# The up stage of a decoder-layer kernel: x1 added late, gathered rows kept out of the first and last round, the final norm in two combined passes

## The reference

```python
# x1: the layer's state after the first sublayer and its norm
def token_block(args):
    xb, eb, gb = args
    act = jax.nn.gelu(jnp.einsum('pd,phkd->phk', xb, expert_down[eb]).astype(f32), approximate=False)
    return jnp.einsum('phk,phkd->pd', (gb * act).astype(x.dtype), expert_up[eb])
# x <- LayerNorm(alpha * x1 + PEER(x1)), alpha = 2 ** 0.25, eps 1e-5
```

## Time and profile before

| | us |
|---|---|
| median of 3 runs | 4306.57 |
| lowest and highest of the 3 | 4306.22 and 4308.96 |
| profiled execution | 4310.81 |
| its span, first to last instruction | 4309.0 |
| TensorE busy | 3957.7 (92%) |
| VectorE busy | 2586.9 (60%) |
| mean granted TensorE clock | 0.958 |

### The profile page before, as it was taken

One profiled execution on the slowest core, in us unless ns is written; L12 is line 12 of the kernel. 1 busy time (PEld: TensorE's weight loads), 2 busy tenths in 40 slices (PEclk: granted clock), 3 DMA queues, 4 the chain that ended last, 5 costly groups with the idle time before them and its releaser, 6 DMA issues. The chain is left out here.

```text
span 4309.0 us, 61280 instructions
## 1 busy us (share of the span) xinstructions
PE 3957.7 (92%) x21744; PEld 3573.4 (83%) x21744; DVE 2586.9 (60%) x5114; ACT 1367.3 (32%) x2139; POOL 1702.3 (40%) x1159
## 2 busy tenths in 40 slices
PE   9999994996888788998999999999988999999996
PEld 7888884886888666998999999999976888888885
DVE  2154102554555334116777888886648888898888
ACT  2133221652222211112472644635512222222220
POOL 0000003624444004000727656566626555555556
PEclk9999996997999899999999999999999999999998
DMA  3223224642222322223549779698888888888884
GB/s 132 97 88 106 94 86 129 160 109 71 76 75 84 138 95 94 88 68 129 136 139 318 231 227 299 201 331 278 262 315 289 289 291 290 285 290 298 280 289 185
DMA packets 390923, 801.82 MB, mean 186 GB/s; under 512 B 65265, under 2 KB 204401, under 8 KB 389745
## 3 DMA queue, kind: packets, MB, share of 16 engines
q1 hardware_dynamic: 280176, 531.25, 36.9%
q0 software_dynamic: 110592, 268.62, 19.9%
HBM read 623.40 MB, written 154.32 MB: 180 GB/s over the span
## 5 line engine op out<-in xcount | busy, mean ns | idle before, releaser
L1935 PE MATMUL r_psd<-x1h,r_dh 128*128 128x384 f32 x2048 | 700.9, 342 | 19.0 <-DVE r_dl L1733 19.0
L1935 PE MATMUL r_psd<-x1l,r_dh 128*128 128x384 f32 x2048 | 688.4, 336 | 0.0
L1935 PE MATMUL r_psd<-x1h,r_dl 128*128 128x384 f32 x2048 | 688.3, 336 | 0.0
L2180 PE MATMUL e_psy<-e_uh,e_Ch 128*128 128x512 f32 x1536 | 600.1, 391 | 36.3 <-DVE e_Cl L2105 31.9
L2180 PE MATMUL e_psy<-e_ul,e_Ch 128*128 128x512 f32 x1536 | 599.5, 390 | 0.0
L2180 PE MATMUL e_psy<-e_uh,e_Cl 128*128 128x512 f32 x1536 | 599.4, 390 | 0.0
L1708 POOL DMA_INDIRECT W<-r_put,r_place x256 | 426.7, 1667 | 405.6 <-DVEq L1882 319.0
L2074 POOL TENSOR_TENSOR e_araw<-e_araw,e_W 128x768 f32<-128x768 f32 x128 | 258.9, 2023 | 401.4 <-DMA e_W<-W 400.5
L1935 PEld LDWEIGHTS r_psd<-x1h,r_dh 128*128 128x128 f32 x2048 | 388.3, 190 | 19.8 <-DVE r_dl L1733 19.8
L1699 POOL DMA_INDIRECT r_rows<-in_down_rows,ids x256 | 262.7, 1026 | 358.8 <-DVE coef L1750 242.8
L2130 DVE SCALAR_TENSOR_TENSOR e_y<-e_rows,coef,e_y 128x1024 f32<-128x1024 f32 x256 | 384.5, 1503 | 15.0 <-DMA e_rows<-in_up,ids 14.9
(11 more groups left out here) (326 smaller groups left out, 7338.3 us busy)
## 6 DMA issues: line engine op xcount, KB each, us to landing
r_draw<-in_down SPq DMA_DIRECT2D x128, 512.0 KB, 5.3
e_uraw<-in_up SPq DMA_DIRECT2D x128, 512.0 KB, 6.2
act<-r_act SPq DMA_DIRECT2D x128, 384.0 KB, 5.0
e_araw<-act SPq DMA_DIRECT2D x128, 384.0 KB, 3.2
e_W<-W SPq DMA_DIRECT2D x128, 384.0 KB, 5.0
W<-r_W SPq DMA_DIRECT2D x32, 1024.0 KB
p_wraw<-in_w_in SPq DMA_DIRECT2D x58, 512.0 KB, 3.7
hT<-p_out SPq DMA_DIRECT2D x58, 512.0 KB, 2.9
```

What stands on the lines that cost most here:

```text
L1935: ins = nc.tensor.matmul(psd[n][:, h, 0:HD], a[c % DEEP][:, k, :], b[:, k, h * HD:(h + 1) * HD], start=(k == 0 and m == 0), stop=(k == KD ...
L2180: ins = nc.tensor.matmul(bank[:], a[s][:, t * P:(t + 1) * P], v[s][:, h * HALF:(h + 1) * HALF], start=(q == 0 and m == 0), stop=(q == G - ...
```

## The change

It is confined to `stage_up`.

- x1 is no longer loaded into `y`. Round 0 copies its banks into `y`, the first two gathered rows are written with a multiply. Each x1 tile is loaded into one new buffer `x` and added, times alpha, at the end of one of rounds 3, 6, ..., 24 (`add_x`).
- Gathered rows by round: none in round 0, 10 in round 1, 8 in most, 9 in rounds 3, 5, ..., 21, 12 in round 30, none in round 31. The first gathers are issued only behind the weigh of chunk 7.
- The norm of a tile is `centre`, (y - mean) * gain, and `finish`, centre * rstd + bias, in halves, both on VectorE. GpSimd only computes the powers. The order in the last round is new, statistics start at bank 0.
- The statistics and the finish of the last tile go by halves, and its two halves are stored apart.
- VectorE's and SyncE's loops are written out. TensorE's and ScalarE's lists are unchanged.

```diff
-    per_round = [NU // NR] * NR
+    per_round = [0, 10] + [8] * (NR - 4) + [12, 0]
+    for n in range(NU - sum(per_round)):
+        per_round[3 + 2 * n] += 1
+    x_round = [3 + 3 * t for t in range(TT)]
...
+        def half(n, h):
+            return y[:, ORDER[n], h * HALF:(h + 1) * HALF]
+        def stats_of(dve, n, h):
             if n >= NG2:
...
+                dve.wait_ge(sem("y_add"), START + BR * (NR - 1) + 2 * (n - NG2) + h + 1)
+            elif h == 0:
                 dve.wait_ge(sem("acc"), START + NU)
...
+            nc.vector.bn_stats(stats[n % 2][:, h, :], half(n, h)).then_inc(sem("stats"), 1)
+        def centre(dve, n):
+            dve.wait_ge(sem("stats"), START + 2 * n + 2)
+            nc.vector.bn_aggr(mv[n][:], stats[n % 2][:]).then_inc(sem("aggr"), 1)
+            dve.wait_ge(sem("aggr"), START + n + 1)
+            nc.vector.tensor_scalar(mv[n][:, 1:2], mv[n][:, 1:2], 1e-5, None, ALU.add).then_inc(sem("var"), 1)
+            dve.wait_ge(sem("ld_ln"), START + 32)
+            nc.vector.scalar_tensor_tensor(y[:, ORDER[n], :], y[:, ORDER[n], :], mv[n][:, 0:1], uraw[0][:],
+                                           ALU.subtract, ALU.mult).then_inc(sem("centred"), 1)
+        def finish(dve, n):
+            dve.wait_ge(sem("rstd"), START + n + 1)
+            dve.wait_ge(sem("centred"), START + n + 1)
             for h in range(2):
...
+                ins = nc.vector.scalar_tensor_tensor(half(n, h), half(n, h), rstd[n][:, 0:1], uraw[1][:, h * HALF:(h + 1) * HALF],
+                                                     ALU.mult, ALU.add)
+                if n == TT - 1:
+                    ins.then_inc(sem("final_last"), 1)
+            if n < TT - 1:
+                ins.then_inc(sem("final"), 1)
...
-            def loads(i):
-                for n in range(2):
-                    sp.wait_ge(sem("C_lo"), START + 2 * i + (n + 1))
-                    load(2 * i + (n + 2), n)
-
-            loads(0)
-            for t in range(TT):
-                sp.dma_start(y[:, t, :], g.x1[t * P:(t + 1) * P, :]).then_inc(sem("ld_y"), 16)
-            with sp.Fori(1, NCH // 2 - 1) as i:
-                loads(i)
+            for c in range(2, NCH):
+                sp.wait_ge(sem("C_lo"), START + c - 1)
+                load(c, c % 2)
+                for t in range(TT):
+                    if c == G * x_round[t]:
+                        sp.wait_ge(sem("x_added"), START + t)
+                        sp.dma_start(x[:], g.x1[ORDER[t] * P:(ORDER[t] + 1) * P, :]).then_inc(sem("ld_y"), 16)
             sp.wait_ge(sem("C_lo"), START + NCH)
             for d, s in ((uraw[0], g.ln2_gain), (uraw[1], g.ln2_bias)):
                 sp.dma_start(d[:], s.partition_broadcast(P)).then_inc(sem("ld_ln"), 16)
-            for n, t in enumerate(ORDER):
-                if n < TT - 1:
-                    sp.wait_ge(sem("final"), START + n + 1)
-                else:
-                    sp.wait_ge(sem("final_last"), START + 1)
+            for n, t in enumerate(ORDER[:TT - 1]):
+                sp.wait_ge(sem("final"), START + n + 1)
                 sp.dma_start(g.out[t * P:(t + 1) * P, :], y[:, t, :]).then_inc(sem("st_out"), 16)
-            sp.wait_ge(sem("st_out"), START + 16 * TT)
+            t = ORDER[TT - 1]
+            for h in range(2):
+                sp.wait_ge(sem("final_last"), START + h + 1)
+                sp.dma_start(g.out[t * P:(t + 1) * P, h * HALF:(h + 1) * HALF], half(TT - 1, h)).then_inc(sem("st_out"), 16)
+            sp.wait_ge(sem("st_out"), START + 16 * (TT + 1))
...
-                if c >= G:
-                    for k in range(NGU // G * (c - G), NGU // G * (c - G + 1)):
-                        gather(k)
             for r in range(NR):
                 for q in range(G):
+                    if r == 0:
+                        for k in range(NGU // G * q, NGU // G * (q + 1)):
+                            gather(k)
                     if r + 2 < NR:
                         weigh(G * (r + 2) + q)
-                    each = per_round[r] // G
-                    for k in range(first_up[r] + each * q, first_up[r] + each * (q + 1)):
+                    for k in range(first_up[r] + per_round[r] * q // G, first_up[r] + per_round[r] * (q + 1) // G):
                         if k + NGU < NU:
                             gather(k + NGU)
             pool.wait_ge(sem("power"), START + 1)
-            pool.wait_ge(sem("ld_ln"), START + 32)
             for n in range(TT):
                 pool.wait_ge(sem("var"), START + n + 1)
-                nc.gpsimd.tensor_tensor(rstd[n % 2][:], mv[n % 2][:, 1:2], power[:], ALU.pow).then_inc(sem("rstd"), 1)
-                if n >= 1:
-                    affine(nc.gpsimd, pool, n - 1, "final")
...
+            def add(r, b):
                 dve.wait_ge(sem("y_mm"), START + BR * r + (b + 1))
                 o = y[:, DENSE[b // 2], b % 2 * HALF:(b % 2 + 1) * HALF]
...
+                bank = psy[(BR * r + b) % NB][:]
+                if r == 0:
+                    ins = nc.vector.tensor_copy(o, bank)
                 else:
                     ins = nc.vector.tensor_tensor(o, o, bank, ALU.add)
                 ins.then_inc(sem("y_add"), 1)
...
+            def accumulate(k):
                 u, n, e = k % NGU, k % NG2, k // NG2
...
+                dve.wait_ge(sem(f"ld_r{u}"), 16 * (k // NGU + 1))
+                if k >= NG2:
+                    dve.wait_ge(sem("acc"), START + k - NG2 + 1)
+                o, scale = y[:, GATHERED[n], :], g.coef[:, n, e:e + 1]
+                if k < NG2:
+                    ins = nc.vector.tensor_scalar(o, rows[u][:], scale, None, ALU.mult)
                 else:
...
+                    ins = nc.vector.scalar_tensor_tensor(o, rows[u][:], scale, o, ALU.mult, ALU.add)
+                ins.then_inc(sem("acc"), 1)
+            def add_x(r, t):
+                dve.wait_ge(sem("ld_y"), START + 16 * t + 16)
+                if t < NG2:
+                    dve.wait_ge(sem("acc"), START + first_up[r] + per_round[r])
+                else:
+                    dve.wait_ge(sem("y_add"), START + BR * r + BR)
+                o = y[:, ORDER[t], :]
+                nc.vector.scalar_tensor_tensor(o, x[:], ALPHA, o, ALU.mult, ALU.add).then_inc(sem("x_added"), 1)
+                dve.wait_ge(sem("x_added"), START + t + 1)
+            for q in range(G):
+                low(0, 0, q)
+            for r in range(NR - 1):
                 done = 0
                 for b in range(BR):
...
+                    add(r, b)
+                    while done < per_round[r] * (b + 1) // BR:
+                        accumulate(first_up[r] + done)
                         done += 1
...
+                    if b % 2 == 1 and b // 2 < G:
+                        low(r + 1, 1 - r % 2, b // 2)
+                if r in x_round:
+                    add_x(r, x_round.index(r))
             for b in range(BR):
...
+                add(NR - 1, b)
+                if 1 <= b <= 4:
+                    finish(dve, b - 1)
+                elif b % 2 == 0 and b > 4:
+                    finish(dve, NG2 + b // 2 - 1)
+                if b < NG2:
+                    done = b
+                elif b == NG2:
+                    done = NG2
+                else:
+                    done = NG2 + b // 2 if b % 2 == 1 else None
+                if b == BR - 2:
+                    stats_of(dve, TT - 1, 0)
+                if done is not None:
+                    for h in range(1 if b == BR - 1 else 0, 2):
+                        stats_of(dve, done, h)
+                    centre(dve, done)
+            finish(dve, TT - 1)
```

More of the change, by code:

```diff
@@ L1974, in stage_up @@
         rows = [sb(f"e_rows{u}", [P, D]) for u in range(NGU)]
[L1975 to L1976 removed]
+        stats, mv = [sb(f"e_stats{u}", [P, 2, 6]) for u in range(2)], [sb(f"e_mv{n}", [P, 2]) for n in range(TT)]
+        rstd, power = [sb(f"e_rstd{n}", [P, 1]) for n in range(TT)], sb("e_power", [P, 1])
         psy = [ctx.enter_context(nc.psum_tensor(f"e_psy{u}", [P, HALF], F32)) for u in range(NB)]
```

82 lines of the change are left out of this document (4 added, 78 removed).

## The result

The changed kernel takes 4345.9 us, median of 4 runs (4338.92 to 4348.51), against 4306.4 of the kernel before: ratio 1.0089, 95% interval 1.0072 to 1.0107. It is slower, by 39 us; the forecast was 4275. The profiled execution took 4348.51 us for a span of 4346.7.

The account below looks back on a forecast made before the run. TensorE bounds the middle of the stage, so gains lie at its start and end: 17.0 + 1.0 + 0 + 13.5 = 31.5 us off the median of 4306.6, so 4275 us; forecast 4269 to 4282, wider range 4265 to 4291.

Parts of the forecast that it names:

- the last sentence on the middle rounds: Middle rounds: after a late eight-row round, the nine-row round has VectorE back in step by bank two; cost 0.
- the replay: Up stage: VectorE's queue stepped through with durations measured before, such as 1.2 us a whole-tile pass, 2.2 us a `low`.
- The 4.16 us from load to weigh: Middle rounds: time from a load's issue at 4220.55 to its weigh at 4224.71, taken from round 30 of before.
- the 5 worked out: Eight-row rounds behind nine-row ones: VectorE stands still about 5 us for a gathered row at bank 5.
- 2.7: Same eight-row rounds: 2.7 us of cover left between the fourth `low` and TensorE's need, so no cost.
- Gathered rows come late: Rival, middle rounds: each microsecond beyond the cover costs one in eleven rounds; slightly late, 3 to 20 us lost, chance 0.16.
- the large one: Rival, middle rounds: rows very late make the kernel slower than before; 4322 at 7 us late, chance 0.04.
- the 1.0 us counted as gained: Start of round 1: a shorter TensorE wait costs 0 to 2.0 us of slow clock, against 2.0; middle taken.
- The start: Round 0: without x1 loads, scalings and gathered rows, TensorE starts round 1 at 3245.2 against 3262.2, 17.0 us earlier.
- The tail: Last round: VectorE needs 40.0 us and sets the end, 4291.9 against 4305.4; 13.5 us gained, including a 1.1 us wait.
- the rivals of fast and slow passes: Tail norm passes: fast, 0.65 us a tile, 4266, chance 0.09; slow, 2.7 us, 4299, chance 0.04.
- The estimate by the rule of the Trainium skill: Tail: each GpSimd power starts only when its centre pass is done, so the last finish comes 0.6 us later.

Follow-up runs that it names:

- one_nine: Changed kernel with nine of the 256 gathered rows left out, so only round 11 has nine rows: 4282.7 us.
- nines_placed: Changed kernel with the accumulates of nine-row rounds placed behind banks 1, 2, 4, 5, 7, 8, 9, 10 and 11: 4322.3 us.
- gathers_first: Changed kernel with the gathers of each slot ahead of its weigh in GpSimd's list, all 256 rows kept: 4280.5 us.
- light_w: Changed kernel loading only the first 64 of the 768 columns of W from chunk 8 on, its own order kept: 4316.6 us.

## Why the prediction was wrong

**The step that failed** is the last sentence on the middle rounds: "The next round, of 9, has VectorE back in step by its second bank". It let every pair of rounds be costed from an undisturbed start. Three things were wrong in it.

- A late `low` isn't over when it has used its cover. It delays a load, the weigh two chunks on and the gathers behind that, which feed the first banks of the next round. In one_nine the lateness of a single one lasted until round 17; the change makes a new one every second round.
- The nine-row round has its own use of the cover. I counted one accumulate more, 1.2 us. But the fifth and sixth row of the round come from the two gathers behind one weigh, and nine rows over twelve banks take them at banks 6 and 7, ahead of the fourth `low`, where eight rows take them at 7 and 8. From rest the round uses 5.3 of 5.5 us, 1.6 of them by a pass of the fourth `low` beside a weigh, for which the replay, with each pass at its own time, had no term.
- The 4.16 us from load to weigh was that of a load at rest. Of the loads whose weigh had been waiting for them (chunks 12 to 119, over 1 us), 24 of 58 had no gather in the 4 us ahead in the kernel before, and 2 of 62 in the changed one; the median went from 5.5 to 7.0 us. For a gather 6.16 us was used; the rows that VectorE waited for came 4.2 to 10.3 us after the issue, 5.9 in the median, so this was fair on the whole and not for the pair ahead of the fourth `low` (5.1 and 7.9).

The wait of VectorE in the eight-row rounds was about right: 4.02 us in nines_placed, and 6.02 in round 12 of one_nine, the round right behind the single one of nine, against the 5 worked out. That TensorE doesn't wait behind it held there too, but with 0.2 us of margin, not 2.7.

**The rival** *Gathered rows come late* named the mechanism, a wait in one round of two, and its sign, with 0.16 for a small form and 0.04 for the large one that came true (4322 there, 4345.9 measured). It put the lateness into the even rounds, where it mostly shows in the odd ones, had neither the circle nor the clock, and its figure for rows 7 us late is 24 us short. The sentence against the large one, that no row of the steady part is near, was no argument: the steady part of before has no shift, so it could not show one, and in the trace of before loads of the steady part do take up to 8.1 us to their weigh (chunk 24, from 3383.05), which the rows shown did not include. The replay should have been run over three rounds on end; its own 5 us wait moved the fourth `low` by 3.4 us, and so the next load and weigh, which was the thing to follow.

**The clock.** The 24.5 us of slow clock had no term behind round 1. TensorE's waits of 2 to 5 us were nearly all followed by a slow stretch. In the 20 us from 3355 on 0.85 was granted, which is 6 us at the lower level of 1.2 GHz and the rest at 2.4, so 3 us lost; behind it 1.00. Over the 11 waits of 1.9 us or more the 24.5 us come to 2.2 each. With them the clock takes two fifths of the loss. Before round 1, too, hardly any of the 1.0 us counted as gained is there: from 3250.95 to 3355.15 it is 104.2 us, less the wait of 4.35 and three rounds of 32.64, 1.9 us, where the 12.95 us wait of before had cost 2.1.

**The start**: forecast 17.0 us, measured 15.6. The replay held: the last `low` ends at 3250.9, 38.3 us behind the first matmul, where it said 37. The 1.4 us arise ahead of the two loads: they leave at 3236.77 and 3239.97, 24.1 and 27.3 us behind the first matmul, where the replay had 22.5 and 25.9. From the second to the end of its e_Cl it takes 10.9 us, where 11.0 was used.

**The tail**: forecast 14.6 us in the cut of the first table, measured 12.9. VectorE begins its last list 8.7 us behind the start of round 31 (7.2 forecast; a row came 1.64 us late in round 30), takes 41.1 us for it (40.0 forecast), and the stores take 3.1 us instead of 3.6. A tile takes 4.75 us from statistics to statistics (4303.18 to 4307.93). Centre takes 1.2 from start to start (1.27 as a duration), for which 1.2 was taken; the finish takes 1.3 from start to start for its two halves (1.41 as a duration), for which 1.2 was taken. The choice of 1.2 between 0.65 and 2.7 holds, and the rivals of fast and slow passes fall. The power is recorded with 1.52 us beside a centre pass, not 0.55, and the last finish waits 0.44 us for it. Its end, 4342.21, comes 0.4 us behind the centre's at 4341.80. The estimate by the rule of the Trainium skill (SBUF — State Buffer, Who interferes with whom), a power that runs only when the centre pass is done, was 0.6 us, and the trace agrees with it, with 0.44: a power of 0.55 us from 4340.69 on would have been done before the centre pass, and nothing would have waited for it.

**With the middle repaired** the forecast stands, for another kernel than the one it was made for: gathers_first measures 4280.5, inside 4269 to 4282, and its stage is 29.8 us shorter than that of before, where 31.5 were forecast.

**What stays open**: why a load right behind gathers takes 3 us longer, also when the mean DMA share is low (light_w), and how the slow clock depends on the length of a wait in detail. The stretched passes beside a weigh were read from the traces, and no run took them out by themselves; they come to 1.6 us in each of eight rounds, 13 us, against 37.3 us of waits. They are there in gathers_first as well (rounds 4, 6 and 10), where no wait comes of them.

## What to carry to other kernels

When a change moves work between rounds of a pipeline whose queues wait for one another, look for the circle (here row, `low`, load, weigh, gather, row) and replay several rounds on end: cover that is spent in one round is missing in the next, and the latencies at rest don't hold once the order has changed. Put requests that only need a free buffer ahead of work that waits for data in an in-order queue; it cost nothing in the kernel before (ratio 0.999 to 1.001), which has slack, and took the circle apart in the changed one. The bound engine's waits should be priced with the slow clock behind them, here about 2 us for each wait of 2 to 5 us.
